# An encoder trunk on one core: the last expert chunk split early, the last down projection, scatter and additions in halves over four banks, and the last norm in a buffer of its own ahead of a branch

## The reference, cut to what matters

```python
for e in range(N_EXPERTS):
    out = out + combine[:, e:e + 1] * swiglu(xt, w1[e], w3[e], w2[e])
...
h = layer_norm(DN_ALPHA * h + f, ln2_w[l], ln2_b[l])
```

## Time and profile before

| | us |
|---|---|
| median of three runs | 1730.88 |
| the three runs | 1730.88, 1726.97, 1731.34 |
| the profiled execution, its own time | 1726.48 |
| its span | 1724.6 |
| one expert chunk, in the steady state (from one chunk's first matmuls to the next's) | 8.41 |
| last matmul group of up(111) released ScalarE at | 1694.49 |
| down(111) began | 1699.48 |
| first statistics of the last norm | 1712.91 |
| last scaling ended | 1721.53 |

### The profile page before, as it was taken

How to read it: one execution, slowest core, us unless ns; L and a number is a source line. 1 busy time by engine, 2 the same in 40 slices (tenths; PEclk the granted TensorE clock), 3 DMA queues, 4 the chain that set the end, 5 groups by cost and what they waited for, 6 DMA issues and landing times.

```text
span 1724.6 us, 18678 instructions
## 1 busy us (share of the span) xinstructions
PE 1650.9 (96%) x7674; PEld 1306.7 (76%) x7674; DVE 1353.5 (78%) x1443; ACT 944.0 (55%) x943; POOL 56.4 (3%) x39
## 2 busy tenths in 40 slices
PE   6998989999999998899999999999999999999995
PEld 4665748988858764788888888888888888888883
DVE  6879456765665945598898998888988989888996
ACT  4312315654310232477777776777777767777772
POOL 0111000000011100000000000000000000000000
PEclk9978989999998978799999999999999999999997
DMA  7221152743433114598988998998989989989870
GB/s 311 98 98 49 74 212 86 270 182 147 173 145 147 49 73 182 208 371 344 375 351 339 372 353 346 366 362 337 364 348 354 361 356 356 360 330 374 350 305 26
DMA packets 40459, 444.23 MB, mean 258 GB/s; under 512 B 4400, under 2 KB 4528, under 8 KB 7216
## 3 DMA queue, kind: packets, MB, share of 16 engines
q1 hardware_dynamic: 39216, 438.78, 65.2%
q10 hardware_dynamic: 1152, 4.19, 0.6%
HBM read 437.71 MB, written 5.24 MB: 257 GB/s over the span
## 4 chain that ended last, share of the span: by engine, by line
PE 84%; DVE 10%; ACT 4%; issue 1%; DMA 0%; DVEq 0%; SPq 0%; ACTq 0%
PE bank L1075 33%; PE bank L1096 15%; PE bank L981 7%; PE bank L583 4%; PE bank L990 3%; PE bank L800 3%; PE bank L587 3%; PE bank L1039 2%; PE bank L753 1%; PE bank L1083 1%; DVE ring_lo L1962 1%; DVE ring_lo L2086 1%; ACT ex_up_hi L1353 1%; PE bank L726 1%; PE bank L1059 1%
## 5 line engine op out<-in xcount | busy, mean ns | idle before, releaser
L1962 DVE TENSOR_TENSOR ring_lo<-ring,ex_up_hi 128x2048 fp32r<-128x2048 f32 x224 | 512.8, 2290 | 50.9 <-ACT ex_up_hi L1353 50.7
L1353 ACT ACTIVATE ex_up_hi<-ring 128x2048 fp32r<-128x2048 f32 x224 | 429.1, 1916 | 115.7 <-PE bank L1075 108.0
L1075 PE MATMUL bank<-ex_up_hi,ex_x_hi 128*128 128x512 f32 x896 | 363.0, 405 | 3.7 <-DVE ring_lo L1962 3.7
L1075 PE MATMUL bank<-ring_lo,ex_x_hi 128*128 128x512 f32 x896 | 350.6, 391 | 0.0
L1075 PE MATMUL bank<-ex_up_hi,ex_x_lo 128*128 128x512 f32 x896 | 349.7, 390 | 0.0
L2086 DVE TENSOR_TENSOR ring_lo<-ring,ex_w_hi 128x2048 fp32r<-128x2048 f32 x112 | 255.5, 2282 | 1.4 <-ACT ex_w_hi L1449 1.4
L1449 ACT ACTIVATE ex_w_hi<-ring 128x2048 fp32r<-128x2048 f32 x112 | 213.4, 1905 | 0.0
L1075 PEld LDWEIGHTS bank<-ex_up_hi,ex_x_hi 128*128 128x128 f32 x896 | 168.3, 188 | 40.9 <-DVE ring_lo L1962 10.8
L1075 PEld LDWEIGHTS bank<-ring_lo,ex_x_hi 128*128 128x128 f32 x896 | 168.2, 188 | 36.2
L1075 PEld LDWEIGHTS bank<-ex_up_hi,ex_x_lo 128*128 128x128 f32 x896 | 168.8, 188 | 30.5
L1096 PE MATMUL bank<-ex_w_hi,ex_mid_hi 128*128 128x512 f32 x448 | 174.4, 389 | 2.1 <-DVE ex_mid_lo L2080 2.1
(11 more groups left out here) (316 smaller groups left out, 2187.7 us busy)
## 6 DMA issues: line engine op xcount, KB each, us to landing
ring<-moe SPq DMA_DIRECT2D x112, 2048.0 KB, 7.6
ring<-moe SPq DMA_DIRECT2D x112, 1024.0 KB, 7.6
ring<-ffn SPq DMA_DIRECT2D x11, 3072.0 KB, 10.9
win<-w_in SPq DMA_DIRECT2D x12, 2048.0 KB, 8.6
win<-w_out SPq DMA_DIRECT2D x4, 2048.0 KB, 10.4
lnb<-ln SPq DMA_DIRECT2D x4, 1024.0 KB, 6.1
tab<-yT ACTq DMA_DIRECT2D x8, 512.0 KB, 5.6
pr<-par SPq DMA_DIRECT2D x2, 1728.0 KB, 12.2
```

The costliest lines, as they stand in the source:

```text
L1075: ins = mm(b[:, :], ex_x[x % 2][x_][:, k, :], (ex_up_hi, lo)[w_][:, k, :], start=(k == 0 and m == 0), stop=(k == KT - 1 and m == 2))
L1353: act(ex_up_hi[:, HS * q:HS * (q + 1), :], wt[:, HS * q:HS * (q + 1), :], ACT.Copy).then_inc(e_uh, 1)
L1962: tt(ring_lo[s][:, half], ring[s][:, half], hi.bitcast(F32), ALU.subtract).then_inc(e_ul, 1)
```

## The change

It does seven things.

1. In the last chunk ScalarE copies w2 in two halves of 1024 columns, ahead of its silu and not behind it, and VectorE subtracts the first half ahead of its multiplication and the second behind it (`w2_lo_half`).
2. The transposes of the last chunk stand between the two halves of down(110) and not behind it. down(111) waits for the first w2 half only, and for the second before its second group.
3. down(111) signals after its first column half (`e_dh`), and `take_y` takes that half then.
4. `scatter_last` writes the four quarters into four banks (6, 7, 4, 5) in the order of `LAST`, both token tiles of the first column half first, and waits for no addition; `add_last` adds them in that order.
5. `last_norm` stands at the end of `all_experts`, ahead of VectorE's branch; its statistics of token tile 0 stand ahead of the fourth addition. It writes to `o`, which lies on `spec` and not on `h`, and scales the second token tile in two halves.
6. SyncE sends the output in three parts: token tile 0, then two column halves of token tile 1 (256 KB each).
7. VectorE's `value_load` moves to the front of the first pass, behind `placed(x0)`. The second pass, if taken, would make the norm again with a Sqrt on ScalarE.

The diff, cut:

```diff
+        o = spec[:, :, :, :].rearrange("p s t n -> p s (t n)")
+        LAST = ((0, 0), (1, 0), (0, 1), (1, 1))
+        LAST_BANK = (6, 7, 4, 5)
...
+        e_lh, e_ll, e_dh = sem("ex_last_w2_hi_half"), sem("ex_last_w2_half"), sem("ex_last_down_half")
+        o_ready, o_sd = sem("out_ready"), sem("out_deviation")
...
                 for g in range(CH + 1, 2 * CH):
                     load_chunk(g)
                 load_last_w2(2 * CH)
-            for t in range(TT):
-                sp.wait_ge(h_ready, 2 * NLN - TT + t + 1)
-                sp.dma_start(out[t * P:(t + 1) * P, :], h[:, t, :]).then_inc(s_out, 16)
-            sp.wait_ge(s_out, 16 * TT)
+                sp.wait_ge(o_ready, 6)
+            sp.wait_ge(o_ready, 1)
+            sp.dma_start(out[0:P, :], o[:, 0, :]).then_inc(s_out, 16)
+            for c in range(2):
+                sp.wait_ge(o_ready, 2 + c)
+                part = slice(c * 512, (c + 1) * 512)
+                sp.dma_start(out[P:2 * P, part], o[:, 1, part]).then_inc(s_out, 16)
+            sp.wait_ge(s_out, 16 * 3)
...
+            def scatter_last(x):
+
+                pe.wait_ge(e_t, x + 1)
+                pe.wait_ge(e_acc, 4 * x)
+                for (t, hf), b in zip(LAST, LAST_BANK):
+                    pe.wait_ge(e_yl, x * 2 + hf + 1)
+                    for n, part in enumerate((y_hi, y_lo)):
+                        ins = mm(bank[b][:, :], place[x % 2][:, t * P:(t + 1) * P], part[:, hf * 512:(hf + 1) * 512],
+                                 start=(n == 0), stop=(n == 1))
+                    ins.then_inc(e_sc, 1)
...
             def down(g):
                 x, c = g // NC_E, g % NC_E
-                pe.wait_ge(e_wl, g + 1)
+                last = g % CH == CH - 1
+                if last:
+                    pe.wait_ge(e_ll, g // CH + 1)
+                else:
+                    pe.wait_ge(e_wl, g + 1)
...
                 for hf in range(2):
                     for f in range(2):
-                        o = f * D + hf * 512
-                        w2 = (ex_w2_hi[g % 2][:, o:o + 512], lo[:, UPW + o:UPW + o + 512])
+                        if last and f and hf == 0:
+                            pe.wait_ge(e_wl, g + 1)
+                        i = f * D + hf * 512
+                        w2 = (ex_w2_hi[g % 2][:, i:i + 512], lo[:, UPW + i:UPW + i + 512])
                         for m, (a, b) in enumerate(SPLIT):
...
+                    if last and hf == 0:
+                        ins.then_inc(e_dh, 1)
+                    if g % CH == CH - 2 and hf == 0:
+                        mid_transposes(g + 1)
                 ins.then_inc(e_dn, 1)
...
-                mid_transposes(b * CH + CH - 1)
                 down(b * CH + CH - 1)
-                scatter(x0 + NE - 1, 0)
-                scatter(x0 + NE - 1, 2)
+                scatter_last(x0 + NE - 1)
...
-                ac.wait_ge(e_dn, x * NC_E + NC_E + 2)
                 for q in range(2):
+                    if x % NE == NE - 1 and q == 0:
+                        ac.wait_ge(e_dh, x // NE + 1)
+                    else:
+                        ac.wait_ge(e_dn, x * NC_E + NC_E + 2)
                     act(y_hi[:, q * 512:(q + 1) * 512], bank[2 * (x % 2) + q][:, :], ACT.Copy).then_inc(e_y, 1)
 
...
                 x0 = b * NE
                 if b:
+                    ac.wait_ge(o_ready, 3)
...
+                    if not more:
+                        ac.wait_ge(w2_in[here], 16 * (g // SLOTS + 1))
+                        ac.wait_ge(e_dn, g + 1)
+                        for f, done_ in enumerate((e_lh, e_wh)):
+                            act(ex_w2_hi[g % 2][:, f * D:(f + 1) * D], ring[here][:, UPW + f * D:UPW + (f + 1) * D],
+                                ACT.Copy).then_inc(done_, 1)
                     ac.wait_ge(e_uu, 2 * g + 2)
                     act(sil[g % 2], bank[4 + g % 2][:, 0:L], ACT.Silu).then_inc(e_sil, 1)
-                    if more:
-                        split_up(1, after)
+                    if not more:
+                        continue
+                    split_up(1, after)
...
             with ac.If(crowded == 1):
                 all_experts(1)
+                ac.wait_ge(ln_var, 2 * NLN + 2)
+                act(rstd, var, ACT.Sqrt).then_inc(o_sd, 1)
...
+            def w2_lo_half(g, f):
+
+                s = MOE_SLOTS[g % SLOTS]
+                if f == 0:
+                    ve.wait_ge(e_lh, g // CH + 1)
+                else:
+                    ve.wait_ge(e_wh, g + 1)
+                part = slice(UPW + f * D, UPW + (f + 1) * D)
+                tt(ring_lo[s][:, part], ring[s][:, part], ex_w2_hi[g % 2][:, f * D:(f + 1) * D].bitcast(F32),
+                   ALU.subtract).then_inc((e_ll, e_wl)[f], 1)
+
+            def add_last(x, n):
+                t, hf = LAST[n]
+                ve.wait_ge(e_sc, x * 4 + n + 1)
+                part = acc[:, t, hf * 512:(hf + 1) * 512]
+                stt(out=part, in0=bank[LAST_BANK[n]][:, :], scalar=comb[:, t, x % NE:x % NE + 1], in1=part,
+                    op0=ALU.mult, op1=ALU.add).then_inc(e_acc, 1)
+
+            def last_norm(b):
+
+                x = b * NE + NE - 1
+
+                def stats(t):
+                    for c in range(2):
+                        ins = nc.vector.bn_stats(bst[:, t, c, :], acc[:, t, c * 512:(c + 1) * 512])
+                    link(ins)
+                    link(nc.vector.bn_aggr(mv[:, t, :], bst[:, t].rearrange("p c s -> p (c s)")))
+                    ts(var[:, t:t + 1], mv[:, t, 1:2], EPS, None, ALU.add).then_inc(ln_var, 1)
+
+                def centre(t):
+                    for c in range(2):
+                        part = slice(c * 512, (c + 1) * 512)
+                        ins = stt(out=o[:, t, part], in0=acc[:, t, part], scalar=mv[:, t, 0:1], in1=lnb[:, part],
+                                  op0=ALU.subtract, op1=ALU.mult)
+                    link(ins)
+
+                def scale(t, a, z):
+                    stt(out=o[:, t, a:z], in0=o[:, t, a:z], scalar=rstd[:, t:t + 1], in1=lnb[:, D + a:D + z],
+                        op0=ALU.mult, op1=ALU.add).then_inc(o_ready, 1)
+
+                take_y_lo(x)
+                for n in range(3):
+                    add_last(x, n)
+                ve.wait_ge(e_acc, 4 * x + 3)
+                stats(0)
+                add_last(x, 3)
+                ve.wait_ge(e_acc, 4 * x + 4)
+                stats(1)
+                ve.wait_ge(s_ln, 16 * NLN)
+                centre(0)
+                if b:
+                    ve.wait_ge(o_sd, 1)
+                    link(nc.vector.reciprocal(rstd, rstd))
+                else:
+                    ve.wait_ge(ln_rstd, 2 * NLN - 1)
+                scale(0, 0, D)
+                centre(1)
+                if not b:
+                    ve.wait_ge(ln_rstd, 2 * NLN)
+                scale(1, 0, 512)
+                scale(1, 512, D)
+
...
                 placed(x0)
+                if not b:
+                    crowded.append(ve.value_load(over[0:1, 0:1], min_val=0, max_val=1))
...
                     if more:
                         up_lo(g + 1, 0, after)
+                    else:
+                        w2_lo_half(g, 0)
                     ve.wait_ge(e_sil, g + 1)
                     tt(mid, sil[g % 2], bank[4 + g % 2][:, L:2 * L], ALU.mult).then_inc(e_pr, 1)
                     if more:
                         up_lo(g + 1, 1, after)
-                w2_lo(b * CH + CH - 1)
+                w2_lo_half(b * CH + CH - 1, 1)
                 mid_lo(b * CH + CH - 1)
-                take_y_lo(x0 + NE - 1)
-                add(x0 + NE - 1, 0)
-                add(x0 + NE - 1, 2)
-                ve.wait_ge(e_acc, 4 * (x0 + NE))
+                last_norm(b)
 
             ve.wait_ge(q_res, 1)
+            crowded = []
             all_experts(0)
-            crowded = ve.value_load(over[0:1, 0:1], min_val=0, max_val=1)
-            with ve.If(crowded == 1):
+            with ve.If(crowded[0] == 1):
                 ts(posx, posx, float(P), None, ALU.subtract).then_inc(q_px, 1)
                 ve.wait_ge(q_px, 2)
                 all_experts(1)
-            layer_norm(4, of(acc), lambda i, t: None)
```

## The result

The changed kernel took 1718.69 us, median of five runs (1717.28 to 1720.93); the kernel before, in five runs on the same chip, 1730.88 (1726.97 to 1731.34). The ratio is 0.9939 with a 95% interval of [0.9924, 0.9953]: 0.6% faster, clear of the 0.3%. The forecast was 1721.0 in a range of 1716.5 to 1726.0.

What follows compares the result with a forecast made beforehand. TensorE bounds the kernel, 96% busy; the change shortens the 30.1 us serial end. Early down and y 3.0, branch 4.0, additions 1.7, less 0.2, output 0.6: 9.1 us off, forecast 1721.0, range 1716.5 to 1726.0.

Steps and rivals of the forecast that it cites:

- w2 and transposes: Last chunk: down(111) begins at 1697.25 and not 1699.48, 2.2 us gained, but lasts 0.1 less without a start from idle.
- The y split: Behind the last down: only one copy and one subtraction remain, 1.35 us where 2.0 stood.
- the additions: Last scatter and VectorE's additions: 4.5 us before, 2.05 for three and 0.75 for the fourth now, 1.7 gained.
- Banks: Last scatter: quarters three and four no longer wait for a bank to be added; counted within the 1.7 us.
- The branch: VectorE's end: flag read and stretch after the branch, 3.98 us, leave the path; the stretch runs beside the last transfer.
- The output: Kernel's end: the last transfer is 256 KB, saving between nothing and 1.3 us, taken as 0.6.
- half scalings: Last norm: two scalings of 512 columns cost 1.41 us where one of 1.28 stood, 0.13 more.
- A: VectorE's branch ends the kernel, behind SyncE; gain 8.1 or 7.8 us; chance 0.07 with over a microsecond lost.
- B: Last chunk: the early start of down(111) doesn't come, 2.2 us lost, gain 6.9, time 1724.0; chance 0.08.
- C: Whole kernel: gain too small to tell or eaten by the runs' spread, 1726.2 to 1727; chance 0.07.
- D: Chunk loop: VectorE's longer program makes each chunk lose time, slower by 0.3% from 0.13 us a chunk; chance 0.03.
- two places: Whole kernel's time before: the three runs shown lie at 1727 and 1731 us; forecast 1721.0 takes both into account.

Runs made afterwards that it cites:

- whole y: Changed kernel with the last y taken only when the whole last down is through; tail 22.1 us against 21.1, last scaling 19.55.
- two banks: Changed kernel with the last scatter in banks 6 and 7 only, quarters three and four waiting for additions; tail 21.5 us against 21.1.
- branch put back: Changed kernel with flag read, branch and norm in the old order, branch ahead of norm; 0.9957 of before, 1721.40 us, tail 24.7.
- sums by ScalarE: Changed kernel with ScalarE making the sums of token tile 1 for VectorE's last norm; 0.9934 of before, 1717.38 us, tail 19.8.
- one output: Changed kernel with the second token tile scaled and sent whole; tail 21.5 us against 21.1, last scaling 18.44.
- shared centring: Changed kernel with token tile 0's centring in the last norm moved from VectorE to ScalarE and GpSimd; 0.9955 of before, tail 22.3 us.
- branch alone: Kernel before with only the early flag read and the last norm ahead of VectorE's branch; 0.9976 of before, tail 26.4 us.
- last down late: Changed kernel with the last chunk's w2 whole behind silu and its transposes behind down(110); tail 23.5 us against 21.1.
- no second pass: Changed kernel without the second pass, its branches and flag reads on all engines; tail 21.0 us against 21.1.
- transposes late: Changed kernel with only the last chunk's transposes put back behind down(110), w2 still early in halves; tail 22.6 us against 21.1.
- read late: Changed kernel with VectorE's flag read behind the last scaling, directly ahead of the branch; tail 21.8 us against 21.1.

## Why the prediction was right

Its positions were counted from the last silu. Predicted and measured:

| step | predicted | measured |
|---|---|---|
| down(111) begins | 2.76 | 2.77 |
| y parts ready | 6.96 | 7.01 |
| first statistics of the norm | 9.0 | 9.02 |
| last scaling ended | 18.56 | 18.58 |
| end of the span | 21.0 | 21.08 |

**w2 and transposes** (2.2 + 0.1): shown, by putting them back, 2.3. **The y split** (0.6, and the earlier first quarter counted with the additions): 1.0 when undone. **Banks**: 0.3 when undone. **The branch** (4.0): 3.65 and 3.7 by the two experiments, each 0.3 short; added alone it was met by a clock that fell earlier, put back it had a stretch of 2.81. **The output** (0.6, less 0.13 for the half scalings): 0.3 to 0.5 when undone, both together. Undone one by one, the parts of VectorE's way to the last scaling are 2.3, 1.0, 0.3 and 3.65, less 0.1, which is 7.1 of the 8.5 measured (27.04 - 18.58). The remaining 1.3 belong to none alone: before, whole y, two banks and the lower clock delayed the additions together, and taking back one leaves the others' cure in place. That account of the 1.3 is argued from the timelines; no run took back all three at once.

**What the sum left out.** It was made in the span, with the 1.9 us between span and time taken as fixed. They became 2.6, so the 9.1 of the forecast is 9.0 in the span and 8.3 in the time. Over the kernels here this distance was 1.8 (before, branch put back, sums by ScalarE), 1.9 (one output), 2.0 (shared centring), 2.1 (branch alone), 2.2 (last down late), 2.3 (no second pass), 2.5 (transposes late), 2.6 (the change, whole y, two banks) and 3.2 (read late); where a kernel ran five times or more, its values lie within 0.2 of each other. So it goes with the kernel and is no chance of the execution. What sets it stays open: VectorE reached its drain 0.5 us ahead of SyncE's signal in the changed kernel and 0.6 in the one with ScalarE's sums, and the distances are 2.6 and 1.8.

**Rivals.** A is refuted in its price but not in its mechanism: the stretch behind the branch is there, 2.9 us, and was 0.5 us from ending the span. The forecast had it through at 1714.9 against SyncE's 1715.1, in its own count; that margin was 0.2 and proved 0.5. The Trainium skill (Runtime: NRT & Kernel Launch, section Instruction fetch mechanics) names code loading behind a taken branch whose target lies outside the loaded code; the runs show the stretch at two places and on two engines, but not what the engine loads in it. B did not come; its margin of 0.3 was 0.35. C did not come: the highest execution of the changed kernel took 1723.2, the forecast of C 1726.2 to 1727. D is refuted: from the first chunk's placing to the last silu it was 983.29 us before and is 983.27 after; the placing there:

```profile
711.75 0.41 DVE L2098 CAST place<-bank 128x256 fp32r<-128x256 f32 x1
```

**Where the number was off.** The median came 2.3 us under the 1721.0. The two medians are 12.2 us apart, and the end of the kernel accounts for 8.3 of them; the other 3.9 were in no term. With the 8.3 alone the median would have been 1722.6, inside the range too, so the range holds without that luck, but that the median came out under the forecast and not over it is luck or an effect that the sum doesn't have. The forecast was also carried to a median that I read as one of two places. Over all runs the kernel before gave 1725.3 to 1733.2, with no two places in it; the changed one 1717.3 to 1723.2. The three runs were too few to tell.

Some of the 3.9 may be an effect. With each kernel's own tail taken from its spans, the last silu began at 1697.4 us in the mean of 42 executions of the kernel before, and at 1696.1 in the mean of 45 executions of the kernels that hold a part of the change or all of it; on each of the four chips of the experiments the second mean was the lower one, by 0.2 to 3.4 us (the 3.4 against a single execution). Nothing in the account would move it, and no run tried to tell an effect of the longer program from chance.

## What to carry to other kernels

When a kernel's bound engine runs out of work, its end is a serial chain and can be added up by the row: count from one event on it, price each operation by the distance to the next and not by its duration, and ask of each step which engine it waits for. A branch past a body of code still costs its engine some 3 us here; in the span it is hidden where it stands behind that engine's last work with a transfer still under way. Read the time beside the span: what a change gives in the one can be partly lost in the other, 9.0 against 8.3 us here. Work taken from the engine that bounds the end pays only if the helper doesn't slow that engine: in the two runs here ScalarE did not, GpSimd did.

## What the runs showed that I had not expected

**The runs' spread lies ahead of the experts, most of it in the two mixers.** In fourteen executions of thirteen kernels the expert stage (first placing to last silu) took 983.1 to 983.7 us, while its beginning lay anywhere between 710.5 and 715.8. Statistics of the norms behind the first mixer, the dense layer and the second mixer, in the timeline of VectorE (the first token tile's, but for the middle row, which is the second's), for the changed kernel at 1718.69:

```profile
251.65 1.29 DVE L1517 BATCH_NORM_STATS2 small<-h 128x6 f32<-128x512 f32 x2
...
473.65 1.29 DVE L1517 BATCH_NORM_STATS2 small<-bank 128x6 f32<-128x512 f32 x2
...
678.53 1.29 DVE L1517 BATCH_NORM_STATS2 small<-h 128x6 f32<-128x512 f32 x2
```

and for the same kernel at 1723.20:

```profile
252.29 1.28 DVE L1517 BATCH_NORM_STATS2 small<-h 128x6 f32<-128x512 f32 x2
...
474.33 1.30 DVE L1517 BATCH_NORM_STATS2 small<-bank 128x6 f32<-128x512 f32 x2
...
682.46 1.29 DVE L1517 BATCH_NORM_STATS2 small<-h 128x6 f32<-128x512 f32 x2
```

From the first row to the second it was 222.00 and 222.04 us, from the second to the third 204.88 and 208.13. Over all fourteen executions, counted from first statistics to first statistics, the first mixer's end lay at 247.2 to 252.3 us, the dense layer took either 218.9 to 219.0 (eight executions) or 220.3 (six), and the second mixer 207.9 to 213.6. The windows of the second mixer, first one execution and then the other (us, PE, PEld, DVE, ACT, POOL busy (x), PEclk, DMA share, GB/s):

```profile
473.65:678.53 204.88, 201.58 (x816) 137.53 (x815) 130.66 (x223) 38.88 (x74) 23.78 (x13) 0.92 0.31 118
```

```profile
474.33:682.46 208.13, 204.84 (x816) 139.38 (x815) 130.61 (x223) 38.87 (x74) 23.80 (x13) 0.90 0.30 116
```

The mean of TensorE's granted clock over that stretch lies between its two levels, 1.2 and 2.4 GHz, at 0.92 and 0.90; in the slower execution it was lower. Whether the clock makes the time or only goes with it, and what sets it, was not tried.

**GpSimd beside VectorE**: a 128x512 operation of two SBUF tensors took 1.88 us beside a 128x1024 multiplication on GpSimd, and 0.74 alone. GpSimd's one-column operation had no such effect: in the changed kernel one of 0.98 us ran from 1708.25, beside the centrings of 1708.09, which took their 1.41.

**A transfer's landing**: the 256 KB parts landed after 2.1 us when the first was issued 2.1 us behind the 512 KB part, after 3.1 and 3.6 when it was issued 0.7 behind it, and in the run with the late read after 2.0 and 2.8 at the first of these distances.
